# A decoder layer's gate projections: seven pairs of gate tiles by seven block products each

## The reference, cut to what matters

```python
h = _rmsnorm(x, mix_norm[l])
proj = h @ w_in[l]
q_sb, k_sb, v_sb, q_d, k_d, v_d, q_x, gates = jnp.split(proj, split_at, axis=-1)
...
g = jax.nn.sigmoid(gates.astype(jnp.float32)).reshape(B, S, N_BRANCH, D).astype(x.dtype)
merged = (g[:, :, 0] * (o_sb @ w_br_sb[l])
          + g[:, :, 1] * (o_dil @ w_br_dil[l])
          + g[:, :, 2] * (o_x @ w_br_x[l]))
x = x + merged @ w_out[l]
```

## Time and profile before

| what | value |
|---|---|
| median of 3 runs | 2163.88 us |
| the profiled execution | 2163.55 us |
| its span in the trace | 2161.7 us |
| PE busy | 2145.2 us |
| DVE busy | 1585.9 us |
| ACT busy | 911.6 us |
| POOL busy | 467.9 us |

### The profile page before, as it was taken

One profiled execution on the slowest core, in us unless ns is written; L12 is line 12 of the kernel. 1 busy time (PEld: TensorE's weight loads), 2 busy tenths in 40 slices (PEclk: granted clock), 3 DMA queues, 4 the chain that ended last, 5 costly groups with the idle time before them and its releaser, 6 DMA issues.

```text
span 2161.7 us, 26377 instructions
## 1 busy us (share of the span) xinstructions
PE 2145.2 (99%) x9968; PEld 1733.1 (80%) x9968; DVE 1585.9 (73%) x1809; ACT 911.6 (42%) x1433; POOL 467.9 (22%) x396
## 2 busy tenths in 40 slices
PE   8999999999999999999999999999999999999999
PEld 7788888888888777777778888888888888888887
DVE  8878888888889787878536343355778888888885
ACT  6333333443445777847442111133333344344433
POOL 3013332323333122221000000002013332333330
PEclk9999999999999999999999999999999999999999
DMA  5211111111113210011112111131111111111113
GB/s 175 63 59 59 51 57 59 59 48 41 59 59 105 88 30 20 20 52 37 40 21 78 49 49 59 49 127 39 49 49 59 59 59 46 43 59 59 56 53 98
DMA packets 47630, 126.55 MB, mean 59 GB/s; under 512 B 4301, under 2 KB 20973, under 8 KB 47248
## 3 DMA queue, kind: packets, MB, share of 16 engines
q1 hardware_dynamic: 45600, 112.61, 16.4%
q10 hardware_dynamic: 912, 10.11, 1.3%
q0 software_dynamic: 992, 2.15, 0.5%
HBM read 116.42 MB, written 9.87 MB: 58 GB/s over the span
## 4 chain that ended last, share of the span: by engine, by line
PE 93%; DVE 4%; ACT 1%; issue 1%; DMA 0%; POOL 0%; SPq 0%; DVEq 0%; ACTq 0%
PE ps L2158 91%; DVE h_lo L1411 1%; DVE tok_lo L1463 1%; PE ps L2781 0%; DVE xT L1759 0%; DVE q_lo L1582 0%; PE ps L2716 0%; DVE h_lo L2070 0%; PE ps L2876 0%; DMA x_nat<-in_x 0%; ACT sb_l L1213 0%; ACT w_hi L896 0%; ACT sb_l L1211 0%; DVE a_lo L1535 0%; DVE w_lo L1404 0%
## 5 line engine op out<-in xcount | busy, mean ns | idle before, releaser
L2158 PE MATMUL ps<-tok_hi,q_hi 128*128 128x512 f32 x1008 | 392.7, 390 | 1.4 <-issue 1.0
L2158 PE MATMUL ps<-tok_lo,q_hi 128*128 128x512 f32 x1008 | 392.2, 389 | 0.0
L2158 PE MATMUL ps<-tok_hi,q_lo 128*128 128x512 f32 x1008 | 392.1, 389 | 0.0
L2158 PE MATMUL ps<-h_hi,w_hi 128*128 128x512 f32 x960 | 370.8, 399 | 1.6 <-ACT h_hi L1133 0.6
L2158 PE MATMUL ps<-h_lo,w_hi 128*128 128x512 f32 x960 | 361.6, 391 | 0.5 <-DVE h_lo L2070 0.4
L1548 DVE TENSOR_TENSOR xT<-xT,ps 128x1024 f32<-128x1024 f32 x252 | 303.4, 1218 | 60.3 <-PE ps L2158 48.9
L2158 PE MATMUL ps<-h_hi,w_lo 128*128 128x512 f32 x960 | 304.2, 390 | 0.0
L2158 PEld LDWEIGHTS ps<-tok_hi,q_hi 128*128 128x128 f32 x1008 | 189.2, 188 | 42.7 <-issue 2.4
L2158 PEld LDWEIGHTS ps<-h_hi,w_hi 128*128 128x128 f32 x960 | 179.9, 188 | 51.6 <-issue 16.3
L2158 PEld LDWEIGHTS ps<-tok_hi,q_lo 128*128 128x128 f32 x1008 | 189.2, 188 | 39.3
L2158 PEld LDWEIGHTS ps<-tok_lo,q_hi 128*128 128x128 f32 x1008 | 189.2, 188 | 39.0
(11 more groups left out here) (309 smaller groups left out, 3705.1 us busy)
## 6 DMA issues: line engine op xcount, KB each, us to landing
raw<-in_weights SPq DMA_DIRECT2D x195, 512.0 KB, 3.5
x_keep<-xT ACTq DMA_DIRECT2D x1, 4096.0 KB, 12.9
x_back<-x_keep ACTq DMA_DIRECT2D x1, 4096.0 KB, 12.2
x_nat<-in_x SPq DMA_DIRECT2D x7, 512.0 KB, 7.4
out<-y_nat SPq DMA_DIRECT2D x7, 512.0 KB, 3.2
toe_keep<-toe_row ACTq DMA_DIRECT2D x2, 704.0 KB, 6.0
m_nat<-in_mem SPq DMA_DIRECT2D x1, 1024.0 KB, 8.1
d_fB<-d_f_keep POOLq DMA_DIRECT2D x2, 512.0 KB, 6.8
```

What stands on the lines that cost most here:

```text
L2158: return pe.matmul(o, a, b, start=start, stop=stop, skip_group_check=True)
```

## The change

Seven pairs of gate tiles, `TWO` = (branch 1: tiles 2-3, 4-5, 6-7; branch 2: tiles 0-1, 2-3, 4-5, 6-7), are now made by seven block products each (`two_gates`). The other ten gate tiles stay as they are. The merge goes branch by branch: the 8 tiles of branch 0, then branch 1, then branch 2; `MERGE` holds the 20 units that are done alone, `TWO_PARTS` the 56 parts of the pairs (49 block products, 7 pairs of branch tiles).

```diff
-MERGE = [(0, b) for b in range(3)] + [(1, b) for b in range(3)]
-MERGE += [(m, 3 + b) for m in range(2) for b in BR_TURN]
-MERGE += [(m, b) for m in range(2, DT) for b in (0, 1, 2, 3, 5, 4)]
+MERGE = [("gate", 0, m) for m in range(6)] + [("branch", 0, m) for m in range(6)]
+MERGE += [("gate", 0, 6), ("gate", 0, 7), ("branch", 0, 6), ("branch", 0, 7)]
+MERGE += [("gate", 1, 0), ("branch", 1, 0), ("gate", 1, 1), ("branch", 1, 1)]
+TWO_PARTS = [part for q in range(len(TWO) - 2) for part in [("gate", q, p) for p in range(SEVEN)] + [("branch", q, 0)]]
+TWO_PARTS += [("gate", q, p) for q in (len(TWO) - 2, len(TWO) - 1) for p in range(SEVEN)]
+TWO_PARTS += [("branch", q, 0) for q in (len(TWO) - 2, len(TWO) - 1)]
```

On PE, a block product and what it waits for:

```diff
+            def two_gates(n):
+                kind, q, p = TWO_PARTS[n]
+                to = bank(2) if p == 5 else bank(3) if p in (1, 3) else bank(q % 2)
+                if p == 0:
+                    if q < 2:
+                        pe.wait_ge(mg_taken, merge_at("gate", 1, 0) + 1)
+                    else:
+                        pe.wait_ge(two_step, SEVEN * (q - 1))
...
+                elif p < 5:
+                    pe.wait_ge(two_kept, 3 * q + p - 1)
+                else:
+                    pe.wait_ge(two_step, SEVEN * q + 3)
+                if p in (1, 2, 4, 6):
+                    pe.wait_ge(factor_step, {1: 6, 2: 13, 4: 10, 6: 14}[p])
+                for j in range(4):
+                    cols = slice(j * P, (j + 1) * P)
+                    mm(to, hi_of[:, cols], factor(p, j, False), j == 0 and p in (0, 1, 5), False)
+                    mm(to, hi_of[:, cols], factor(p, j, True), False, False)
+                    last = mm(to, lo_of[:, cols], factor(p, j, False), False, j == 3)
```

On ACT, for each block product one rounding, and a copy out of PSUM (p = 0, 1, 2) or a sigmoid of half a tile (p = 3 to 6):

```diff
+            def two_keep(n):
...
+                act.wait_ge(part_done, NPART + n + 1)
+                act.wait_ge(gated_sum, 8 if q == len(TWO) - 1 else 2 * q + (1, 2, 2)[p])
...
+                nc.scalar.activation(to, bank_of, ACT.Copy).then_inc(two_kept, 1)
...
+            for n in range(NTWO):
+                if n:
+                    two_keep(n - 1)
+                if n + 4 < NTWO:
+                    two_round(n + 4)
+                elif n + 4 - NTWO < AHEAD:
+                    split_hi(U_OUT + n + 4 - NTWO)
+                if n:
+                    two_sigmoid(n - 1)
```

On DVE, four sums of blocks of h (`factor_sum`, ten operations 2048 wide) and their rests (`factor_rest`, four more in six instructions), and then the list around the pairs:

```diff
+                if c == 7:
+                    factor_sum(1, 0, rounded(0, 1), rounded(0, 0), ALU.subtract)
+                elif c == 9:
+                    factor_sum(1, 1, t_full[1], rest(0, 1), ALU.add)
...
+            dve.wait_ge(h_half_read, 1)
+            factor_sum(4, 0, rounded(1, 0), t_full[2], ALU.subtract)
+            two_rest(0)
+            two_rest(1)
+            factor_sum(4, 11, t_full[4], rest(1, 0), ALU.add)
+            factor_rest(2, 2, 11)
+            gate_scale(1, 1)
+            two_rest(2)
+            two_rest(3)
+            gate_branch(1, 1)
+            factor_rest(4, 4, 12)
+            for n in range(NTWO):
+                if n:
+                    two_add(n - 1)
+                if n + 4 < NTWO:
+                    two_rest(n + 4)
+                elif n + 4 - NTWO < AHEAD:
+                    split_lo(U_OUT + n + 4 - NTWO)
+                if n == NTWO - 2:
+                    for k in range(2):
+                        merged_lo(k)
+            two_add(NTWO - 1)
             for m in range(2, DT):
...
                 merged_lo(m)
```

POOL makes the four weight sums of each pair, and SP loads two units and half a unit (`rows`, the branch weights) for each:

```diff
+            def two_sums(q):
...
+                after_half(pool, two_part("gate", q, 1))
+                after_two(pool, q, 0, 1)
+                nc.gpsimd.tensor_tensor(s1, a21, a22, ALU.add).then_inc(w_summed, 1)
+                pool.wait_ge(w_summed, base + 1)
+                nc.gpsimd.tensor_tensor(a21, s1, a11, ALU.subtract).then_inc(w_summed, 1)
...
+            for q in range(len(TWO)):
+                for half in range(2):
+                    if q == 0:
+                        sp.wait_ge(split_done, U_OUT + half - 1)
+                    else:
+                        sp.wait_ge(part_split, NPART + two_part("gate", q - 1, (4, 6)[half]) + 1)
+                    sp.dma_start(raw[:, half, :], weights[two_at(q) + half]).then_inc(raw_in[half], 16)
```

More of the change, by code:

```diff
@@ new lines, in factor_round, with two_round @@
+            def factor_round(i, step):
+                act.wait_ge(factor_step, step)
+                for first, part in t_hi[i]:
+                    last = nc.scalar.activation(part, t_full[i][:, first:first + part.shape[1], :], ACT.Copy)
+                last.then_inc(factor_hi, 1)
+            def two_round(n):
+                kind, q, p = TWO_PARTS[n]
+                after_half(act, n)
+                if kind == "branch":
+                    act.wait_ge(rows_in, 16 * (q + 1))
+                    w = two_width(q)
+                    nc.scalar.activation(two_hi(n)[:, 0:w], rows[:, 0:w], ACT.Copy).then_inc(part_hi_done, 1)
+                    return
+                after_two(act, q, 0 if p < 5 else 1)
+                if p in (1, 3, 4):
+                    act.wait_ge(w_summed, W_SUMS + 4 * q + {1: 1, 3: 3, 4: 4}[p])
+                    src = two_sum(n)
+                elif p == 2:
+                    act.wait_ge(w_summed, W_SUMS + 4 * q + 2)
+                    src = raw[:, 0, T1]
+                else:
+                    src = raw[:, p // 5, BOTH[p // 6]]
+                nc.scalar.activation(two_hi(n), src, ACT.Copy).then_inc(part_hi_done, 1)
@@ new lines, in factor_sum, with rest, rounded, factor_rest @@
+            def factor_sum(i, step, a, b, op):
+                if step:
+                    dve.wait_ge(factor_step, step)
+                nc.vector.tensor_tensor(t_full[i], a, b, op).then_inc(factor_step, 1)
+            def rest(half_d, half_t):
+                return part_of_h(h_lo, half_d, half_t).bitcast(F32)
+            def rounded(half_d, half_t):
+                return part_of_h(h_hi, half_d, half_t).bitcast(F32)
+            def factor_rest(i, turn, step):
+                dve.wait_ge(factor_hi, turn)
+                dve.wait_ge(factor_step, step)
+                for first, part in t_hi[i]:
+                    ks = slice(first, first + part.shape[1])
+                    last = nc.vector.tensor_tensor(t_lo[i][:, ks, :], t_full[i][:, ks, :], part.bitcast(F32), ALU.subtract)
+                last.then_inc(factor_step, 1)
@@ new lines, in two_rest @@
+            def two_rest(n):
+                kind, q, p = TWO_PARTS[n]
+                dve.wait_ge(part_hi_done, NPART + n + 1)
+                w = two_width(q) if kind == "branch" else 512
+                if kind == "gate" and p == 1:
+                    dve.wait_ge(w_summed, W_SUMS + 4 * q + 2)
+                if kind == "branch":
+                    src = rows[:, 0:w]
+                elif p in (1, 3, 4):
+                    src = two_sum(n)
+                elif p == 2:
+                    src = raw[:, 0, T1]
+                else:
+                    src = raw[:, p // 5, BOTH[p // 6]]
+                nc.vector.tensor_tensor(two_lo(n)[:, 0:w], src, two_hi(n)[:, 0:w].bitcast(F32), ALU.subtract).then_inc(part_split, 1)
@@ L2110, in _ @@
[L2110 to L2122 removed]
+            gate_scale(0, FILL + 1)
@@ L2842, in _ @@
             pe.wait_ge(d_biased, DN)
-            gate_part(1, 1)
+            gate_part(0, FILL)
             pe.wait_ge(d_pT_ready, DN)
-            gate_part(1, 2)
-            branches(0)
-            branches(1)
-            for m in range(2, DT):
-                for b in range(3):
-                    gate_part(m, b)
-                branches(m)
+            gate_part(0, FILL + 1)
+            for kind, b, m in MERGE[FILL + 2:]:
+                if (kind, b, m) == ("gate", 1, 1):
+                    gate_part(b, m, 0, DT // 2).then_inc(h_half_read, 1)
+                    gate_part(b, m, DT // 2, DT)
+                elif kind == "gate":
+                    gate_part(b, m)
+                else:
+                    branch(b, m)
@@ L2854, in _ @@
+            for n, (kind, q, p) in enumerate(TWO_PARTS):
+                pe.wait_ge(part_split, NPART + n + 1)
+                if kind == "gate":
+                    two_gates(n)
+                else:
+                    two_branch(n)
             for m in range(DT):
```

477 lines of the change are left out of this document (329 added, 148 removed).

## The result

The changed kernel takes 2151.94 us (median of 5 runs, 2151.61 to 2152.64) against 2163.88 us. The ratio is 0.9944, with a 95% interval of 0.9930 to 0.9959: faster by 11.9 us (0.6%), where 16.6 were forecast. The direction was right, but the time lies 0.4 us above the top of the range (2151.5). Its profiled execution took 2151.61 us with a span of 2149.6 us.

The account below looks back on a forecast made before the run. PE's matmuls were taken to bound the kernel: 2163.55 - 19.05 (matmuls) + 1.5 (entry) + 1.0 (seam) = 2147.0 us profiled; with the median 0.33 above, the forecast was 2147.3 us, range 2144.3 to 2151.5.

Parts of the forecast that it names:

- The matmuls: On PE in the merge: seven pairs save 84 matmuls at 0.2268 us each, 19.05 us, the whole gain.
- the old seam: Start of the output projection before the change: first output tile took 12.18 us for 10.89 of matmuls, 1.3 us lost.
- The steady part: Pairs after the first: added DVE, ACT and POOL work hides beside PE, DVE at 70 to 75%; cost 0.
- the handover through the shared gate tiles: Between pairs: ACT's copy of the second block product waits for the last pair's branch sums; claimed hidden, 4 us free.
- The second and third rival: Second: POOL and DVE block in every pair, about 2155, chance 0.12; third: late handover through shared gate tiles, 2168, chance 0.03.
- the wider spacing: Fourth rival, PE in the pairs: fewer matmuls but spaced wider, a third of the gain lost, 2153.7; chance 0.03.
- The stretch: A 2048-wide DVE operation beside a POOL sum takes 3.38 instead of 2.28 us, 1.1 more; half of it was added.
- The seam: Start of the output projection: second output tile starts after 13.2 us against 12.18, 1.0 us more; bounds -1.3 to +3.
- the walk: Step-by-step dating of the engines' work at the entry and at the seam; PE waits about 1.0 us at the entry.
- The entry: Last stage ahead of the pairs: PE's third block product waits for ACT's copy; 1.5 us, bounds 0 to 4.
- A: Start of gate tile (1, 0), from which the entry is dated; third block product due at A + 29.95, copy at A + 31.0.
- The first rival: Entry and seam: nothing is lost at either end, 2144.8, or 2143.5 if the old 1.3 goes too; chance 0.15.

## Why the prediction was right or wrong

- **The matmuls (19.05 us): right.** With both losses taken away, 19.4 us are gained, 0.9 of them the old seam: 18.5 of the 19.05, if the rest is theirs. The spacing stayed 0.2268: 500.77 us for 2208.
- **The steady part (0): right.** No wait in 150 us, DVE at 72% where 70 to 75% were worked out, and the handover through the shared gate tiles never waited. The second and third rival, and the wider spacing, fall. So POOL's sums beside DVE cost nothing there. The stretch itself is in the steady part as well (there the 512-wide rests of loaded weights take 0.96 us on average, against 0.69 alone), but DVE has room for it.
- **The seam (1.0 us): right**, 1.13 measured, by the steps of the walk.
- **The entry (1.5 us, bounds 0 to 4): the step that failed**, a term of the sum that was mis-sized. The mechanism was right: the third block product waits for ACT's copy behind DVE's list. It cost 3.84 + 1.6 = 5.4 us. Two things were wrong in it.
  - The stretch was taken by half, "POOL's sums fall beside DVE's 2048-wide work [...]; I add half of it". By the walk's dates DVE's two wide operations ran from A + 22.6 and POOL was free for its next two sums from A + 21.9, so by these dates they meet, and there was no reason for a half. The two operations took 3.37 and 3.39. POOL's first two sums, priced at 2.9 together, took 3.7 from start to end, with DVE reading beside them (1.77 for a 512-wide rest), and began 0.4 later than dated. The walk's 1.0, 0.4 and 0.8 for these two and 2.2 for the stretches make 4.4; the steps around them gave 0.6 back.
  - The clock was not in the sum at all. All rows before had it at 1.00, but they had no wait of PE longer than 0.4 us in the stretches that I read, so they could say nothing on a clock behind a longer one. The upper bound of 4 us was about the wait alone; with the clock behind it, it would have been 5.6, and the range would have held the time.
  - The range itself was also added up short. The bound is 1.0 + 3.3 = 4.3, written as 4, and even 4 with the 3 of the seam gives 2163.88 - 19.05 + 7 = 2151.8, not 2151.5; with 4.3 it is 2152.1. A range up to there would have held the time by luck only, because the seam left most of its 3 us unused: the entry cost 5.4, beyond its own bound.
- **The first rival** (nothing lost at either end, 2144.8) did not happen. With the other orders the time is 2144.80, but that it agrees so closely is chance, since 0.9 us of the old seam went there too.

## What to carry to other kernels

When work of a steady scheme is made ready in a last stage before it starts, that stage is the tightest place, not the steady part: price each DVE operation there with the stretch by any POOL operation that the dates put beside it, in full. A wait of PE by a few microseconds may cost its length and then about 1.6 us more, by matmuls at the lower clock behind it. Before a wait is cured by holding back the disturber, look at who is queued behind the consumer of what is held back; a later place for work that nobody needs yet cured it here, a later sum did not.

## What the runs showed of the hardware that was not expected

The granted clock can fall to its lower level behind a single wait in a kernel that is otherwise 99% busy on PE: it fell at waits of 3.7, 2.6 and 4.7 us, each time for some three microseconds (1.6, 1.5 and 1.7 us lost), and stayed up at waits of 1.5, 2.4 and 3.4 us. It came down 1 us after the end of the wait in one execution of the changed kernel, 0.1 us after it in another, and before the end of the wait of 2.6 us. Two 512-wide POOL operations and two 2048-wide DVE operations side by side took what they would take one after the other (7.07 us from 1230.59 to 1237.66, against 2 x 1.29 + 2 x 2.28 = 7.14), and a 16-column POOL operation beside the same DVE operation costs it 0.03 us.
